# Attention stages of a decoder block: where the two halves of a query tile are scaled and split

## The reference

```python
h = _rms_norm(x, norm_attn_g[l])
proj = h @ w_in[l]
qa, ka, va, fa, qb, kb, vb, ga, gb = jnp.split(proj, split_points, axis=-1)
oa = _fox_attention(qa..., ka..., va..., log_f)          # 8 heads of 64, causal, with a forget bias
qb, kb = _partial_rope(qb), _partial_rope(kb)
ob = _dilated_mixture(qb, kb, vb)                        # 12 heads: windows 128/512/2048, dilation 1/4/16
mixed = jax.nn.sigmoid(ga) * (oa @ w_branch_a) + jax.nn.sigmoid(gb) * (ob @ w_branch_b)
x = x + mixed @ w_out[l]
x = x + jnp.square(jax.nn.relu(rms_norm(x) @ w_up[l])) @ w_down[l]
return _rms_norm(x, norm_final_g)
```

## Time and profile before

| | |
|---|---|
| time of the runs, median (lowest to highest) | 1677.96 us (1674.87 to 1681.14) |
| time of the profiled execution | 1677.7 us |
| its span, first to last instruction | 1675.9 us |
| mean granted TensorE clock | 0.98 of full |
| attention stages and the mixing between them | 71 to 686 us |
| busy: PE / DVE / ACT over the span | 93% / 65% / 47% |

### The profile page before, as it was taken

One profiled execution on the slowest core, in us unless ns is written; L12 is line 12 of the kernel. 1 busy time (PEld: TensorE's weight loads), 2 busy tenths in 40 slices (PEclk: granted clock), 3 DMA queues, 4 the chain that ended last, 5 costly groups with the idle time before them and its releaser, 6 DMA issues. The chain is left out here.

```text
span 1675.9 us, 20825 instructions
## 1 busy us (share of the span) xinstructions
PE 1552.0 (93%) x7436; PEld 1277.8 (76%) x7436; DVE 1094.3 (65%) x1775; ACT 782.0 (47%) x1396; POOL 4.1 (0%) x20
## 2 busy tenths in 40 slices
PE   6998888897789998899999999999999899999997
PEld 5777677775677786788888887888888677777776
DVE  5687878866566666523225567666666677777776
ACT  6466666662556656511113454343343444444442
POOL 0000000000000000000000000000000000000000
PEclk9999999999899999999999999999999999999998
DMA  5210100110010201111211543444444784444412
GB/s 176 89 39 26 38 26 26 28 37 13 13 51 26 76 26 36 36 48 44 56 55 55 151 126 94 151 144 167 163 149 151 248 285 138 140 138 144 139 39 101
DMA packets 161584, 154.45 MB, mean 92 GB/s; under 512 B 7048, under 2 KB 126920, under 8 KB 161360
## 3 DMA queue, kind: packets, MB, share of 16 engines
q1 hardware_dynamic: 161488, 153.19, 28.9%
HBM read 115.35 MB, written 37.81 MB: 91 GB/s over the span
## 5 line engine op out<-in xcount | busy, mean ns | idle before, releaser
L942 PE MATMUL ps<-hspl,wsp 128*128 128x512 f32 x1536 | 428.9, 414 | 5.4 <-ACT tmp L1356 3.7
L942 PEld LDWEIGHTS ps<-hspl,wsp 128*128 128x128 f32 x1536 | 270.8, 193 | 52.2 <-ACT tmp L1356 4.6
L1233 PE MATMUL ps<-dn_b,a_hi 128*128 128x512 f32 x896 | 280.0, 394 | 17.5 <-DVE keep L2022 11.8
L898 PE MATMUL ps<-hspl,wsp 128*128 128x512 f32 x960 | 220.7, 390 | 1.4 <-DVE keep L1869 1.4
L1233 PEld LDWEIGHTS ps<-dn_b,a_hi 128*128 128x128 f32 x896 | 168.0, 189 | 59.3 <-issue 24.1
L898 PEld LDWEIGHTS ps<-hspl,wsp 128*128 128x128 f32 x960 | 179.7, 188 | 38.6 <-issue 1.6
L1233 PE MATMUL ps<-dn_b,a_lo 128*128 128x512 f32 x448 | 175.8, 392 | 0.0
L2022 DVE TENSOR_TENSOR keep<-keep,ps 128x512 f32<-128x512 f32 (+1 forms) x144 | 101.5, 713 | 38.2 <-PE ps L1233 24.5
L1233 PE MATMUL ps<-up_b,a_hi 128*128 128x512 f32 x384 | 119.6, 393 | 3.7 <-DVE up_b L2022 2.7
L1855 DVE TENSOR_TENSOR work<-ps,work 128x128 fp32r<-128x128 f32 (+3 forms) x144 | 59.1, 420 | 72.3 <-ACT work L1401 70.2
L1604 ACT ACTIVATE keep<-keep 128x512 f32<-128x512 f32 x64 | 40.5, 633 | 125.9 <-DVE keep L2184 42.8
(11 more groups left out here) (211 smaller groups left out, 2560.8 us busy)
## 6 DMA issues: line engine op xcount, KB each, us to landing
hidden<-keep SPq DMA_DIRECT2D x112, 256.0 KB, 2.2
dn_raw<-hidden SPq DMA_DIRECT2D x56, 512.0 KB, 6.4
raw<-in_w_in SPq DMA_DIRECT2D x47, 512.0 KB, 3.8
a_raw<-in_w_up SPq DMA_DIRECT2D x36, 256.0 KB, 3.0
a_raw<-in_w_down SPq DMA_DIRECT2D x32, 256.0 KB, 3.0
spare<-in_w_down SPq DMA_DIRECT2D x32, 256.0 KB, 4.2
spare<-in_w_up SPq DMA_DIRECT2D x28, 256.0 KB, 3.2
keep<-in_x SPq DMA_DIRECT2D x8, 512.0 KB, 7.0
```

Source lines behind the costliest of these rows:

```text
L898: ins = pe.matmul(ps[:, cols], w(wp, k), mv(mp, k)[:, cols], start=(k == 0 and n == 0), stop=(k == ks - 1 and n == 2))
L942: ins = pe.matmul(psp(u, g), wsp[c % 2][:, wp, k * P:(k + 1) * P], hspl[:, mp, k, cols], start=(n == 0), stop=(n == 23), skip_group_check= ...
L1233: ins = pe.matmul(o, a_part(n, j, wp, k), b_block(n, j, mp, k), start=(first and k == 0 and m == 0), stop=(k == ks - 1 and m == 2), skip_g ...
```

## The change

```diff
 # ScalarE, mixer_steps
-                    if G < last and G // 2 + 1 < BLOCKS * MIX:
-                        query_hi(G // 2 + 1, G % 2)
                     if G < last:
                         exps(G)
                     if first <= G - 1 < last:
                         probs_hi(G - 1)
                     if G < last:
+                        for B, n in query_ops(G):
+                            query_hi(B, n)
                         if s == 1:
                             values_hi(t)
 # ScalarE, ahead of stage 0
             raw_evacuate(0, 5)
+            query_hi(1, 0)
             mixer_steps(0, STEPS * N_DIL)
 # VectorE, mixer_steps
-                    if G < last and G // 2 + 1 < BLOCKS * MIX:
-                        query_lo(G // 2 + 1, G % 2)
+                    if G < last:
+                        for B, n in query_ops(G):
+                            query_lo(B, n)
 # VectorE, ahead of stage 0
             query_lo(0, 1)
+            query_lo(1, 0)
             mixer_steps(0, STEPS * N_DIL)
```

More of the change, by code:

```diff
@@ L185, in key_tiles @@
     return [(i - 1, None), (i, None)]
+def query_ops(G):
+    B, n = (G + 1) // 2 + 1, (G + 1) % 2
+    if G % STEPS == 13 or G == STEPS * N_DIL - 1 or B >= BLOCKS * MIX:
+        return []
+    return [(B, 0), (B, 1)] if G % STEPS == 14 or G == STEPS * N_DIL else [(B, n)]
 def tiles_of(G):
```

## The result

The changed kernel takes 1683.33 us (median of 6 runs, 1682.26 to 1686.72); the kernel before takes 1678.62 in runs beside it (1673.76 to 1681.14). The ratio is 1.0042, with an interval of 1.0026 to 1.0058. So the change makes the kernel slower by 5 to 7 us, where I had said 0.9 us faster: the medians differ by 4.7, and the ratio, which is not the quotient of the two medians, comes to 7. The profiled execution has a span of 1684.9 us, 9.0 more than before; it is the longest of its six.

What follows compares the result with a forecast made beforehand. It took VectorE's chain as the bound in stages 2 to 4, PE's query waits there as slack. Terms +6.4 - 4.8 + 0.5 + 0 - 2.2 - 0.8 = -0.9 us gave 1677.0 us; 8-in-10 range 1664 to 1688.

Steps and rivals of the forecast that it cites:

- the mechanism and its size per step: PE's query waits vanish; VectorE's low half instead waits for ScalarE's high half, 0.35 us a step in stages 2 to 4.
- stage 5: Last dilated stage: no rotations, so VectorE has room and the new wait stays off the path; 1.9 us gained.
- rival 1: VectorE's new wait is short, so stages 2 to 4 give 2 us each: sum -13.3, 1664.7 us; chance 0.22.
- stage 1: Dilated stage without a new wait: removing PE's 1.73 us query wait at step 10 and its slow clock gains 2.0 us.
- slack in stages 2 to 4: Steps 3 to 12: VectorE runs without gaps, so giving back PE's 1.0 us query wait per block gains nothing.
- what absorbs: Stages 2 to 4: existing waits take up 0.7, 1.0, 0.6 and 0.5 to 0.8 us of lateness, leaving +6.4 us.
- the way into fox: Mixing, steps 96 and 97: two query halves behind one exponential, the next maximum queued behind them; +0.5 us.
- this ring: Stages 6 and 9: the chain maximum, exponential, cast, low part, query, next maximum is the bound.
- Stages 6 and 9: Fox stages with fewer projections: -0.8 us for stage 6 and -2.2 us for stage 9.
- Stages 7 and 8: Fox: PE's longer wait for the bank copy and the vanished query waits cancel; net 0, each -1.5 to +1.5 us.
- rival 3: Slower: VectorE's new wait lands undiminished, +13 us in stages 2 to 4; sum +8.9, 1687 us; chance 0.13.
- Rival 2: PE's query waits really come back, 41.8 + 4.9 us and some 3 us of slow clock: 1628 us; chance 0.05.

Runs made afterwards that it cites:

- e7_short: Changed kernel, but ScalarE's query high half reads and writes 256 contiguous columns instead of strided ones: 1671.68 us, ratio 0.9974 to the kernel before.
- e1_ahead: Changed kernel, but ScalarE's query high half goes back ahead of the exponential, still a step early: 1656.12 us, ratio 0.9891 to the kernel before.
- e3_fox: Kernel before, with the change in the fox stages only: 1674.07 us, ratio 0.9995.
- e2_dilated: Kernel before, with the change in the dilated stages only: 1687.86 us, ratio 1.0069.
- e9_both: Changed kernel, with ScalarE's high half ahead of the exponential and VectorE's low half one step later, behind the maximum: 1635.70 us, ratio 0.9754 to the kernel before.
- e8_behind: Kernel before, same steps, but ScalarE's query high half moved behind the exponential and the cast: 1695.55 us, ratio 1.0119.

## Why the prediction was right and wrong, point by point

**Right: the mechanism and its size per step.** PE's waits for the query are gone, VectorE's new wait is there, and in stage 3 it makes a step 0.35 us longer, as I took it. The row at VectorE's line shows a little less (0.31 in the mean of stages 2 to 4), and only with stage 5 are there 15.7 us in all. By the rule of the Trainium skill that I had weighed (ScalarE: Activation LUTs, section "What ACT_TABLE_LOAD costs") the high half should take 0.40 us, an estimate from that page; that is right for operands that lie side by side (0.417 in `e7_short`) and wrong for the strided ones (0.655). The wait of almost nothing that I took from it holds for the short half (0.4 us in stages 2 to 5 of `e7_short`). So `e7_short` is rival 1 made real. It takes 1671.68 us beside 1675.33, where I had put rival 1 at 1664.7: stages 2 to 4 gave 1.6 us together and not the 6 of that rival, stage 1 gave 0.9 and stage 5 lost 0.4, where 2.0 and 1.9 of gain were in its sum.

**Right: slack in stages 2 to 4**, up to step 10. `e1_ahead` shows no gain in steps 4 to 8 of stage 3, and 0.2 us by step 10; in stage 4 it gains nothing up to step 13. **Mis-sized: what absorbs.** I had +6.4 us for these stages and measured +9.1. I had carried stage 3 well up to step 10 (2.3 us late, measured 2.35); it came out 3.1 late and not 2.0. A part of it is a lateness that I did not carry over the stage's end: the copy of the last projection group now stands behind the two halves of step 14 and the later steps, and PE waits for it in step 0 of stage 4. These are PE's rows there, and a window over them:

```profile
290.63 0.75 PE L950 MATMUL ps<-hspl,wsp 128*128 128x512 f32 x2 [2.48 <-ACT tmp L1364]
291.46 2.91 PE L950 MATMUL ps<-hspl,wsp 128*128 128x512 f32 x6
```

```profile
290.00:296.00 6.00, 5.37 (x19) 4.39 (x20) 3.83 (x11) 3.20 (x10) 0.00 (x0) 0.72 0.23 69
```

The granted clock is 0.72 over these 6 us, and the six matmuls take 2.91 us where the same six take 1.63 at the full clock. My 0.5 to 0.8 us of slack between the last low part and the value transposes was counted as if only that chain ended the stage: nothing was absorbed there, and the exponentials go from 2.65 us late at step 15 to 3.12 at step 2 of stage 4. Stage 4 (+3.6 for my +2.4) has a granted clock of 0.57 over 4 us behind a wait of 2.09 us for the exponential at step 11, where the kernel before has 1.00.

**Wrong: stage 5, the largest miss.** I had -1.9 us, "so VectorE has room and the new wait stays off the path"; it came at +2.1, and +0.5 for the way into fox as predicted. The step that failed is the reading of VectorE's gaps as room. (From my -0.9 us to the +9.4 of the table are 10.3 us; stage 5 has 4.0 of them, stages 2 to 4 2.7, stage 1 1.7 and the start 1.5.) The timeline of one step, ScalarE and PE:

```profile
366.40 0.26 ACT L1409 CAST work<-ps 128x128 fp32r<-128x128 f32 x1
...
366.68 0.66 ACT L1384 ACTIVATE work<-tmp 64x256 fp32r<-64x256 f32 x1
```

```profile
366.56 0.33 PE L1001 MATMUL ps<-ident,tmp 128*128 128x128 f32 x1 [0.43 <-ACT tmp L1399]
```

and VectorE:

```profile
366.69 0.29 DVE L1864 TENSOR_TENSOR work<-ps,work 128x128 fp32r<-128x128 f32 x1 [0.68 <-ACT work L1409]
367.37 0.60 DVE L1837 SCALAR_TENSOR_TENSOR work<-tmp,work 64x256 fp32r<-64x256 f32 x1 [0.39 <-ACT work L1384]
...
367.88 0.29 DVE L1857 CUSTOM_DVE_ANT_0 ps<-ps,dil_bias 128x128 f32<-128x128 f32 x1
```

VectorE idles for 0.68 us and then for 0.39, and yet it has no room. The gap of 0.68 ends with the cast, the cast stands behind the exponential, and the exponential needs the last maximum of VectorE. The next maximum follows right behind the low half. With no side jobs left the step is a ring of maximum, exponential, cast, low part, query, maximum, and a wait inside a ring is part of its length. I had named this ring for stages 6 and 9 and not looked for it in stage 5. The second table bears it out: the changed kernel needs 0.92 us more for four steps, and the short half takes this away (10.45). With the high half ahead of the exponential they are 1.11 shorter than before (9.36). That gain comes in one step, at step 6, where in the kernel before ScalarE's copies waited for PE's projections, and VectorE's outputs and the next maximum for these copies:

```profile
354.42 0.58 ACT L1356 COPY tmp<-ps 128x512 f32<-128x512 f32 x1 [0.95 <-PE ps L942]
```

```profile
355.42 0.60 DVE L1869 TENSOR_TENSOR keep<-ps,o_part 64x256 f32<-64x256 f32 x1 [1.02 <-ACT o_part L1416]
```

In `e1_ahead` PE has no wait for the query ahead of these projections, and neither idle time is there. The ring is not the whole miss of 4.0 us. Counted from step 2 as in the table, but only up to the last exponential of stage 5, the changed kernel is at +1.6 us, the short half at -0.6 and `e1_ahead` at -1.9, which is what I had forecast. So the wait for the high half has 2.2 us of the miss, and the rest of ScalarE's order 1.4. The last 0.4 come in the mixing behind the stage, where nothing is changed. PE waits 3.09 us there in every kernel; over 4 us behind that wait the granted clock was 1.00 before and 0.64 in the changed kernel.

**Wrong: stage 1** (-2.0 predicted, -0.3). The wait of the earlier trace rows did come back (`e1_ahead` has -1.6, close to the forecast; 0.9 of such a gain can be the clock alone, which is what `e3_fox` has in stage 1 with the order of before, see below), but ScalarE's order, at which I had put nothing here, took it. The new wait for the high half itself is small as forecast: 0.12 us once, up to step 7. But the high half of 0.42 now stands ahead of the weight split, the key stack and the copy for the outputs, and at step 8 the exponential is 0.53 us late, at step 10 0.87 (in `e1_ahead` 0.00 and -0.24). ScalarE and VectorE at steps 7 to 8:

```profile
147.39 0.42 ACT L1384 ACTIVATE work<-tmp 64x256 fp32r<-64x256 f32 x1
147.83 1.06 ACT L1287 CAST wsp<-raw 128x1024 fp32r<-128x1024 f32 x1
148.91 0.37 ACT L1424 COPY o_part<-ps 64x256 f32<-64x256 f32 x1
```

```profile
149.31 0.42 DVE L1878 TENSOR_TENSOR keep<-ps,o_part 64x256 f32<-64x256 f32 x1 [0.31 <-ACT o_part L1424]
```

and at steps 9 to 10, where the key stack takes 2.06:

```profile
151.01 0.42 ACT L1384 ACTIVATE work<-tmp 64x256 fp32r<-64x256 f32 x1
151.45 2.06 ACT L1372 CAST work<-tmp 64x1024 fp32r<-64x1024 f32 x1
```

```profile
153.54 2.01 DVE L1829 TENSOR_TENSOR work<-tmp,work 64x1024 fp32r<-64x1024 f32 x1 [0.52 <-ACT work L1372]
...
157.40 0.43 DVE L1878 TENSOR_TENSOR keep<-ps,o_part 64x256 f32<-64x256 f32 x1 [0.41 <-ACT o_part L1424]
```

I had counted this in fox and, with 0.3 us, in stage 3, but not here.

**Fox: partly right.** Stages 6 and 9 (-0.8, -2.5) are where I put them (-0.8, -2.2), and the wait for the bank takes the place of the query's, as forecast. For stage 9 the match is real (`e3_fox` has -2.5 too), but the sum did not have all of it: behind a wait of 2.00 us for the query at step 10 the granted clock before was 0.65 over 4 us, and the changed kernel has no such wait there. For stage 6 it is not: `e2_dilated`, unchanged there, has -0.8 as well, and `e3_fox`, changed only there, +0.4. Between executions that stage moves with the clock behind a wait of 2.55 us, which the kernel before and `e2_dilated` both have: over the 5 us behind it the granted clock was 0.50 in the one and 0.66 in the other. So nothing of my -0.8 is confirmed; that it matches is luck. Stages 7 and 8, of the same work, part: -0.5 and +1.0, within my bounds; the rows are in the last section.

**Mixing and start.** +0.5 for the way into fox was right. Of the +1.5 at the start 0.8 is there before the first scores, thus not from the change, and 0.65 is VectorE's low half waiting in step 0 for the high half behind the exponential, at which I had put "cost nothing" looking at the two instructions ahead of the stage alone. (And 158 halves of each kind are moved, not 160: the two of the first block stay ahead of stage 0.)

**The rivals.** The time fell between the forecast and rival 3. Rival 3 had the right sign and the right place, but not the right size: stages 2 to 4 have +9.1 us of its 13, and the rest is from stages 5 and 1, where the gains that it counted did not come. Rival 2, that the waits come back, at which I had put 0.05 and some 50 us, is what `e9_both` comes near to: 39.6 us against 1675.33 beside it. For this change it could not come about, because the change added a wait; the argument that I had used against it, that VectorE has no gap, was true of the order before and not of the work. VectorE had 0.24 us a step to give.

## What to carry to other kernels

When an instruction is moved to another step, price its new place in the in-order queue apart from the step: what its consumer does meanwhile, and what is queued behind it. Here the step gave 1.1% and the place took 1.5%. And an idle gap of an engine is room only if what ends it does not depend on that engine's own last result; follow the releaser back once round before calling it slack. A good use of such a gap is an instruction whose operands are ready a whole step ahead, as the low half in `e9_both`.

## What the runs showed of the hardware

**The same wait costs the clock in one execution and not in the next.** `e3_fox` runs stage 1 with the order of before and has the wait of the earlier trace rows again, 1.74 us instead of 1.73:

```profile
154.92 0.50 PE L994 MATMUL ps<-work 128*128 128x256 f32 x2 [1.74 <-DVE work L1842]
```

A window of 4 us behind it, first of the kernel before, then of `e3_fox` (behind the busy times of the five engines stands the granted clock):

```profile
154.60:158.60 4.00, 3.94 (x13) 3.14 (x14) 3.05 (x8) 2.75 (x7) 0.00 (x0) 0.60 0.00 1
```

```profile
154.60:158.60 4.00, 3.68 (x20) 3.11 (x21) 3.28 (x10) 3.03 (x7) 0.00 (x0) 1.00 0.01 4
```

In the one the clock was 0.60 of full, between 1.2 and 2.4 GHz, in the other it stayed full, and from these scores to those of the next step it took 2.41 us instead of 3.88. Over the whole stage 0.9 us of that is left. Within the changed kernel, at step 9 of stages 7 and 8, PE waits for the copy out of the bank:

```profile
531.28 0.73 PE L950 MATMUL ps<-hspl,wsp 128*128 128x512 f32 x2 [2.27 <-ACT tmp L1364]
...
598.64 1.22 PE L950 MATMUL ps<-hspl,wsp 128*128 128x512 f32 x2 [2.28 <-ACT tmp L1364]
```

```profile
531.00:535.00 4.00, 3.72 (x23) 3.28 (x24) 3.50 (x7) 3.10 (x7) 0.00 (x0) 1.00 0.00 0
...
598.00:602.00 4.00, 3.36 (x11) 2.83 (x12) 3.28 (x6) 2.80 (x8) 0.00 (x0) 0.57 0.49 130
```

Stage 8 came out 1.5 us worse than stage 7; in `e7_short`, with the same order in fox, both have +1.0 and +1.1. The Trainium skill (TensorE: Matmul & The Clock Gate, section "HAM oscillation — how this bites in real kernels") says that waits of PE bring the half clock. The rows agree that they can, and add that one of this length may or may not. `e8_behind` has waits of 2.85 us in stage 3 and 2.88 in stage 4; over 4 us behind them the granted clock was 1.00 and 0.57. And the wait of 3.09 us (3.08 in some) in the mixing, which is the same in all ten kernels run, left the clock at 1.00 in two of them (the kernel before and `e3_fox`), while the other eight had 0.57 to 0.67 behind it. What decides was not tried. For the reading it means that a stage's time from one profile is uncertain by 0.9 to 1.5 us where such a wait stands in it, and that I should have counted the clock of the earlier trace rows as a chance and not as a fixed cost.

**Strided reads on ScalarE.** The same 64x256 instruction takes 0.655 us (median of the 64 in stages 2 to 5 of the changed kernel; the 0.649 of its row mixes in the 32 short ones of stages 0 and 1) when it reads every fourth or sixteenth token, and 0.417 when the columns lie side by side. VectorE's subtraction, which reads the same tokens, takes 0.60 in stages 2 to 5 and 0.42 in the other stages.
